# First blocks of the first two layers' projections: two row tiles in banks of their own, turned features ahead of the last early step, and the weight chunk split behind the first features

## The reference

```python
def rms_norm(x, gain):
    y = xf * lax.rsqrt(jnp.mean(xf * xf, axis=-1, keepdims=True) + EPS)
    return (y * gain).astype(x.dtype)

def modulate(x, gain, shift, scale):
    return rms_norm(x, gain) * (1 + scale) + shift
...
    h_l = modulate(x, norm_mix[i], mod_l[0], mod_l[1])
    h_c = modulate(ctx, norm_mix[i], mod_c[0], mod_c[1])
    # i == 0: even_mixer (gated linear attention and attention), i == 1: odd_mixer
    m_l, m_c = even_mixer(h_l, h_c, ev_w_in[j], ev_w_out[j], ...)
    x = x + mod_l[2] * m_l
```

## Time and profile before

| | before |
|---|---|
| median of 3 runs | 1868.26 us (1864.27 to 1869.49) |
| profiled execution | 1866.97 us, of which the span is 1865.1 us |
| PE busy | 1662.8 us, 89% of the span |
| DVE busy | 1117.2 us, 60% |
| ACT busy | 1037.8 us, 56% |
| DMA | 348.05 MB, mean 187 GB/s |
| early modulation (start to `mod_ready`) | 0 to 37.84 us |
| first block of in0 starts | 47.52 us |
| out0 starts | 375.11 us |
| first block of in1 starts | 747.75 us |

### The profile page before, as it was taken

One profiled execution on the slowest core, in us unless ns is written; L12 is line 12 of the kernel. 1 busy time (PEld: TensorE's weight loads), 2 busy tenths in 40 slices (PEclk: granted clock), 3 DMA queues, 4 the chain that ended last, 5 costly groups with the idle time before them and its releaser, 6 DMA issues.

```text
span 1865.1 us, 22644 instructions
## 1 busy us (share of the span) xinstructions
PE 1662.8 (89%) x8804; PEld 1273.4 (68%) x8804; DVE 1117.2 (60%) x1746; ACT 1037.8 (56%) x1865; POOL 155.3 (8%) x157
## 2 busy tenths in 40 slices
PE   4998789897899993899899999988999899999988
PEld 2776447774677772767677777757878667777766
DVE  1225685435688886774589996436754565355453
ACT  4224326625688884385677765526655546446573
POOL 1000100003000003100004331000010010000000
PEclk9999879998899996999899999996999989999999
DMA  8345688012999994301487773530055214414511
GB/s 333 136 157 190 228 335 349 1 68 96 349 422 421 422 387 191 114 1 46 172 322 294 286 288 110 195 138 1 1 190 184 110 49 173 173 68 170 183 65 46
DMA packets 54425, 348.05 MB, mean 187 GB/s; under 512 B 5680, under 2 KB 5680, under 8 KB 18480
## 3 DMA queue, kind: packets, MB, share of 16 engines
q1 hardware_dynamic: 48128, 323.15, 45.6%
q0 software_dynamic: 6192, 23.46, 3.2%
HBM read 317.23 MB, written 29.36 MB: 186 GB/s over the span
## 4 chain that ended last, share of the span: by engine, by line
PE 64%; DVE 15%; ACT 11%; DMA 6%; issue 2%; POOL 1%; SPq 0%; POOLq 0%; DVEq 0%; ACTq 0%
PE bank L1402 15%; PE bank L1404 14%; PE bank L1403 14%; DMA ring_float<-weights_dram 5%; DVE ring_float32r L2891 3%; PE bank L1435 2%; ACT ring_high L725 2%; DVE ring_float32r L2384 2%; DVE Z_float32r L2891 2%; PE bank L1632 1%; ACT hT_float L773 1%; ACT arena_float L860 1%; PE bank L1621 1%; PE bank L1786 1%; PE bank L1916 1%
## 5 line engine op out<-in xcount | busy, mean ns | idle before, releaser
L2384 DVE TENSOR_TENSOR ring_float32r<-ring_float,ring_high 128x1024 fp32r<-128x1024 f32 x206 | 245.5, 1227 | 309.3 <-ACT ring_high L725 308.9
L725 ACT ACTIVATE ring_high<-ring_float 128x1024 fp32r<-128x1024 f32 x206 | 209.4, 1061 | 272.1 <-DMA ring_float<-weights_dram 270.2
L1402 PE MATMUL bank<-ring_high,x_float32r 128*128 128x512 f32 x608 | 242.2, 398 | 6.3 <-DVE mix_float32r L2423 3.3
L1403 PE MATMUL bank<-ring_float32r,x_float32r 128*128 128x512 f32 x608 | 238.7, 393 | 0.0
L1404 PE MATMUL bank<-ring_high,mix_float32r 128*128 128x512 f32 x576 | 226.4, 393 | 0.0
L2891 DVE TENSOR_TENSOR ring_float32r<-ring_float,ring_high 128x1024 fp32r<-128x1024 f32 x122 | 154.4, 1312 | 31.2 <-ACT ring_high L880 31.2
L1402 PE MATMUL bank<-ring_high,arena_float32r 128*128 128x512 f32 (+1 forms) x404 | 156.5, 387 | 18.4 <-DVE arena_float32r L2413 5.1
L2891 DVE TENSOR_TENSOR Z_float32r<-Z_float,arena_float32r 128x1024 fp32r<-128x1024 f32 x126 | 163.0, 1338 | 12.6 <-ACT arena_float32r L880 12.3
L1404 PE MATMUL bank<-ring_high,arena_float32r 128*128 128x512 f32 (+1 forms) x404 | 153.7, 381 | 0.0
L1403 PE MATMUL bank<-ring_float32r,arena_float32r 128*128 128x512 f32 (+1 forms) x404 | 153.4, 380 | 0.0
L1402 PEld LDWEIGHTS bank<-ring_high,x_float32r 128*128 128x128 f32 x608 | 114.1, 188 | 40.1 <-issue 5.2
(11 more groups left out here) (421 smaller groups left out, 3196.2 us busy)
## 6 DMA issues: line engine op xcount, KB each, us to landing
ring_float<-weights_dram SPq DMA_DIRECT2D x216, 1024.0 KB, 4.8
Z_float<-weights_dram SPq DMA_DIRECT2D x63, 1024.0 KB, 7.5
sent<-post_row SPq DMA_DIRECT2D x1, 11776.0 KB, 39.2
Z_float<-sent SPq DMA_DIRECT2D x23, 512.0 KB, 9.1
made<-mix_float POOLq DMA_DIRECT2D x21, 512.0 KB, 7.9
post_row<-norm_post_dram POOLq DMA_DIRECT2D x4, 512.0 KB, 4.5
small<-small_dram SPq DMA_DIRECT2D x1, 1072.0 KB, 9.1
x_float<-x_dram SPq DMA_DIRECT2D x1, 1024.0 KB, 5.3
```

What stands on the lines that cost most here:

```text
L725: nc.scalar.activation(ring_high[:, slot, half], ring[:, slot, half], ACT.Copy).then_inc(high_ready, 1)
L1402: nc.tensor.matmul(out, left[0], right[0], start=start, stop=False)
L1403: nc.tensor.matmul(out, left[0], right[1], start=False, stop=False)
L2384: ve.tensor_tensor(ring_low[:, slot, half], ring[:, slot, half], ring_high[:, slot, half], ALU.subtract).then_inc(low_ready, 1)
```

## The change

- `lead_pool`: in the first block of a projection with four row tiles, tiles 0 and 1 go to `CARRY` (banks 6 and 7) and tiles 2 and 3 to `A`. This holds for in0, out0 and in1.
- `project` takes a bank just ahead of a tile's first product, in all blocks of all projections.
- `mod_early`: eight `dense` products ahead of the first step and five behind each step. The first four feature turnings are issued ahead of the last step, and the other four stay behind the last turn.
- ACT copies the first step's result ahead of the last row tile's normalization, and splits the first chunk of in0 behind the first features rather than ahead of them. DVE splits it likewise behind the first low part.

```diff
+        def lead_pool(n, T, t):
+            return CARRY if n == 0 and T == NT and t < 2 else A
...
-            def drain(*copies, func=ACT.Copy):
-                b = A.filled_bank(act)
+            def drain(*copies, func=ACT.Copy, pool=A):
+                b = pool.filled_bank(act)
...
-                i.then_inc(a_free, 1)
+                i.then_inc(pool.free, 1)
...
                     n.then_inc(a_free, 1)
+                    if j == 0 and between:
+                        between()
...
-                            drain((dst(t), lambda b, w=w: b[:, 0:w], scale(t), None))
+                            drain((dst(t), lambda b, w=w: b[:, 0:w], scale(t), None), pool=lead_pool(n, T, t))
...
+                if i == 0:
+                    mod_copy(mod_rows_early, 1)
                 normed(NT - 1)
                 if i == 0:
-                    mod_copy(mod_rows_early, MOD_EARLY)
+                    mod_copy(mod_rows_early, MOD_EARLY - 1)
                     seen.next(mod_ready)
-                    chunk_high(STREAM["in0"][0])
-                modulate(i, 0, NT, "first")
+                modulate(i, 0, NT, "first", (lambda: chunk_high(STREAM["in0"][0])) if i == 0 else None)
...
             def mod_early():
                 pe.wait_ge(mod_cleared, 1)
-                for _ in range(MOD_EARLY):
+                keep_active(bank[7], 8)
+                for n in range(MOD_EARLY):
+                    if n == MOD_EARLY - 1:
+                        seen.next(normed_ready, NT)
+                        transposes(mix, NT, 0, 4)
                     mod_step(mod_rows_early)
+                    keep_active(bank[7], 5)
                 mod_turn(mod_rows_early).then_inc(mod_turned, 1)
...
-                    banks = [A.take(pe) for _ in range(tiles)]
+                    pools = [lead_pool(n, tiles, t) for t in range(tiles)]
+                    banks = []
                     rows_per = KT // (w // 256)
                     for k0 in range(0, KT, rows_per):
                         last = k0 + rows_per == KT
                         high, low = split_chunk(rows_per)
                         for t in range(tiles):
+                            if k0 == 0:
+                                banks.append(pools[t].take(pe))
...
                             if last:
-                                i.then_inc(a_full, 1)
+                                i.then_inc(pools[t].full, 1)
...
-                seen.next(normed_ready, NT)
-                transposes(mix, NT)
+                    transposes(mix, NT, 4)
+                else:
+                    seen.next(normed_ready, NT)
+                    transposes(mix, NT)
...
                 project("first", T, [(T, 512)] * 2)
+                CARRY.drained(pe)
                 keep_active(bank[6], 20)
...
-            def features_low(name, T):
+            def features_low(name, T, between=None):
...
                         signal(ve.tensor_tensor(low[:, ks, :], hT[:, ks, :], high[:, ks, :], ALU.subtract), act_low)
+                    if j == 1 and between:
+                        between()
...
-                        dve.wait_ge(a_free, whole["y", i, n, t])
+                        dve.wait_ge(*whole["y", i, n, t])
...
-                if i == 0:
-                    chunk_low(first)
-                features_low("first", NT)
+                features_low("first", NT, (lambda: chunk_low(first)) if i == 0 else None)
```

More of the change, by code:

```diff
@@ L754, in normed, with features @@
                 nc.scalar.activation(mix[:, t, :], x[:, t, :], ACT.Copy, scale=rstd[:, t:t + 1]).then_inc(normed_ready, 1)
-            def features(T, scale_bias=None, split=None):
+            def features(T, scale_bias=None, split=None, between=None):
                 per = 4 // T
@@ L991, in route_exps, with modulate @@
                     nc.scalar.activation(src[:, 0:4 * T], src[:, 0:4 * T], ACT.Exp).then_inc(route_out, 1)
-            def modulate(i, which, T, split=None):
-                features(T, lambda k, s: (modA[:, i, which, k, s:s + 1], modT[:, 48 * i + 24 * which + k, s:s + 1]), split)
+            def modulate(i, which, T, split=None, between=None):
+                features(T, lambda k, s: (modA[:, i, which, k, s:s + 1], modT[:, 48 * i + 24 * which + k, s:s + 1]), split, between)
             def first_layer(i):
@@ L1035, in after @@
                 def after(n, t):
-                    whole["y", i, n, t] = A.drains
+                    pool = lead_pool(n, T, t)
+                    whole["y", i, n, t] = pool.free, pool.drains
                     if n == 0 and t == T - 1:
@@ L1457, in mod_late, with transposes @@
                     mod_step(mod_rows_late)
-            def transposes(src, T):
+            def transposes(src, T, first=0, last=KT):
                 per = 4 // T
-                for j in range(KT // per):
+                for j in range(first // per, last // per):
                     b = A.take(pe)
```

## The result

The kernel took 1852.91 us after the change (median of 8 runs, 1849.41 to 1858.59), and 1864.26 us before it (8 runs, 1857.61 to 1869.49, three of them known to the forecast). The ratio is 0.9942, 95% interval 0.9924 to 0.9961: 11.4 us are gained, 7 to 14 by the interval. The profiled execution has a span of 1850.1 us where it was 1865.1. Of the experiments' runs one of e1 took 3219.74 us, where its five others took 1850.73 to 1853.41, and it is in none of the ratios.

The account below looks back on a forecast made before the run. The prediction took PE as the bound, where it idles or runs at its lower clock. Gains of 3.4 + 1.8 + 1.9 + 0.9 + 1.2 = 9.2 us from 1866.97 gave 1857.8, stated as 1858, range 1853.5 to 1863.

Parts of the forecast that it names:

- Early modulation: Steps before in0: dense products raise the clock sooner and the DMA allows the faster steps; 3.4 us gained.
- The third rival: Early steps: chunks land as late as before, only block starts gain; sum 5.8 us, 1861.2 us; chance 0.12.
- Start of in0: From mod_ready to the end of the first chunk's products: earlier products, slow clock stretch left in; 1.8 us gained.
- the slow stretch: Behind a block's start: PE at the lower clock level for a while, costing 1.7 us; left in by the forecast.
- Start of out0: First block of out0: PE goes on when its turnings end; 1.9 us gained, up to 3.6 without slow stretch.
- its second block: Out0's second block: no more wait for ACT to drain the fourth tile; 0.9 us gained.
- Start of in1: First block of in1: 2.4 us gained without a slow stretch, 0.7 with it; 1.2 us taken.
- The first rival: Block starts: short waits keep the clock low, costing 1.7 us at three places; 1862.9 us; chance 0.13.
- The fifth rival: In0 and out0: their slow stretches vanish too, 1.6 + 1.7 us more gained; 1854.5 us; chance 0.13.

Follow-up runs that it names:

- e1: Changed kernel without the early-modulation edits and the chunk's new place; banks 6 and 7 and the late bank take kept: 1852.59 us, ratio 0.9927.
- e8: The changed kernel run again, nothing altered: 1851.28 us, ratio 0.9918.
- e6: Changed kernel with in0's first chunk split ahead of the features again, as before: 1853.54 us, ratio 0.9927.
- e3: Kernel before with only the bank take moved to just ahead of each tile's first product, all in pool A: 1852.17 us, ratio 0.9925.
- e11: Kernel before with only the bank take moved, all in pool A, run a second time: 1852.97 us, ratio 0.9917.
- e5: Kernel before with eight dense products in the idle time ahead of in0, out0 and in1, banks taken as before: 1863.34 us, ratio 0.9986.
- e12: The kernel before, profiled a second time, nothing altered: 1861.38 us.
- e4: Changed kernel without its 28 dense products in the early modulation: 1851.5 us, ratio 0.9918.
- e9: Kernel before with the bank take moved, four turnings ahead of the last early step and the early copy, no dense products: 1850.66 us, ratio 0.9914.
- e10: Kernel before with the bank take moved and six dense products ahead of in0 and in1: 1854.01 us, ratio 0.9917.
- e2: Changed kernel with the early edits kept, but four banks taken ahead of each block in pool A as before: 1863.0 us, ratio 0.998.
- e7: Changed kernel computing only one of four thin products per early half step, sums incomplete: mod_ready at 36.45 us, no whole time given.

## Why the prediction was right or wrong

**Early modulation, 3.4 us: wrong.** This is the step that failed, by the largest amount. It measured 0.4 (37.84 to 37.47), and even that is no more than the scatter of `mod_ready` among profiles with the same code up to there (36.67 to 38.66 over seven). The failing sentence is "The DMA allows it: ... six more at 2.4 to 2.6 us". The chunks came every 2.8 to 3.2 us (15.75, 21.34, 27.45, 33.91, two chunks between each). The rate was read at 14 to 16 us, among loads that had all been issued at the start, and carried over to chunks that each wait for a slot. There 333 to 368 GB/s were seen over ten microseconds before and 340 to 348 after, and only here and there more (407 from 14 to 24 us in e8). Neither bound of the term allowed for this, and why the rate is lower there stays open. The third rival, that chunks land as late as before, came true with a reason that its text did not have: it let the DMA's full share speak for it, and the share was indeed 0.91 after and 0.97 before from 24 to 34 us. The clock did rise, at 14.8 us where the forecast had 15.5.

**Start of in0, 1.8 us: right in size** (2.05, from 22.52 to 20.47), with the slow stretch kept as chosen. The chunk's low part was to end 7.3 us behind `mod_ready`, and PE waited for it until 7.2 behind. What the forecast didn't ask is whether the chunk's new place was worth having. Split first, in0 gains 3.5 (e6), or 4.2 to 4.5 without the other early edits too (e1, e3, e11). By the first product the new place costs 0.7. The rest of these differences is the slow stretch, which reaches further into the products in the kernel after.

**Start of out0, 1.9, and its second block, 0.9: the place right, the size short.** The first product came 2.1 sooner and the second block's wait is gone, but the two kernels differ by 4.5 (52.73 less 48.24, with the missing record). The rest is the slow stretch, 1.7 in the forecast's account and 1.35 by e5. The forecast had priced it nearly rightly (1.9, 0.9 and 1.7 make 4.5) and let it stay; it went. That is the second step that failed.

**Start of in1, 1.2: short by the same.** The whole block gained 2.50. The forecast had 2.4 for a start without a slow stretch, and that is what came. So over out0 and in1 it is 3.0 us short.

**The first rival, a clock that falls in small waits,** did not come in the kernel after, with waits of 0.32 us in in1's first tile and a clock of 1.00 from 740 us on in both of its profiles. It did come once in ten profiles with an early `take`, in e1, for 1.3 us at one place where the forecast had 1.7 at three. The Trainium skill (TensorE: Matmul & The Clock Gate, "A second HAM failure mode") tells of a clock that swings behind short idles between groups. One fall like it was seen here in ten profiles, and none in the kernel after.

**The fifth rival** came half: of the two that it names, out0's stretch vanished and in0's stayed, and in1's, which it doesn't name, vanished as well. So the stages gave 0.4 + 2.05 + 4.5 + 2.5 = 9.4 us in the profile. That this is near the forecast's 9.2 is luck: 3.0 us too much in the early modulation stand against 3.2 too little at the starts.

**The base.** The forecast took these from 1866.97, the profiled execution. That was 3 us above a usual one in a stretch far from the change (e12), and above the 1864.26 of the result's 8 runs of before. (The median of the three runs known then, 1868.26, was higher still.) 1864.26 less 9.4 would be 1854.8, 1.9 above what was measured. So the forecast missed its range for the base, 2.7 too high, and for these 1.9, and not for its sum. The medians of the experiments differ by more than the stages explain: 12.2 to 17.0 us for e1, e3, e4, e6, e8, e9, e10 and e11, where the sums over in0, out0 and in1 are 9 to 11.5. No stage of their profiles has another gain in common beside that of 1170 to 1330 us, which all but e9 have, and e2, e5 and e12 too. So 2 us of the gain (e3) up to 5 (e8) are not assigned, in e9 over 7, and whose they are stays open. The sets differ by such amounts without the `take` as well: e2 is 2.8 faster with nothing gained at the starts, and e5 is 2.4 faster with 4.5 gained there. Of the 15.0 us between the two profiles' spans, 3.35 are the stretch from 1170 to 1330 us and 3.0 another, from 900 to 1000 us, where the granted clock is 0.95 before and 1.00 after. E8, the same kernel as after, has none of these 3.0. Two single runs of the same kernel differ by 7.7 us (e12).

## What to carry to other kernels

Take a bank just ahead of the product that needs it, not all banks ahead of a block. That move alone gave here as much time as the whole change (1852.17 and 1852.97, against 1852.91 and 1851.28), 11.4 us at the three starts (e3). Of these 4.5 are, by e5, the clock that no longer falls behind an idle PE, and the rest the earlier products and out0's second block. Where a start must wait, a few `dense` products in the wait bring back the clock's part alone (1.35 to 1.56 us a start). Read a DMA rate where loads are issued as in the stage that it is to bound: ten microseconds from 8 us on would have shown 426 GB/s, and ten from 24 on, where each load waits for a slot, 368. Take a forecast's base from the median of more than three runs, with a second profile where stretches far from the change may have been unlucky.

## What the runs showed of the hardware

Idle time of PE ahead of a full stretch is paid twice, and the second part comes later: 1.86 us of idling ahead of out0 brought the clock down not in the gap but behind it, while PE was fully busy (0.57 at 376 to 378 us, 0.58 at 378 to 380, and 1.00 again from 380). Dummy products in the gap gave all of this back (e5). In1's waits of 0.32 us left the clock up in nine of ten profiles, and in one it fell behind them (e1).

Work moved ahead of a wait can cost more than it saves. With half of the turnings gone from behind the last turn, PE was idle for 4.53 us in e9 and had the lower level from 40 to 46 us, and in the kernel after from 38.7 to 48.9 (in e7, with the same turnings moved, only from 39.8 to 43.2); e3, with all turnings behind the turn, had its slow stretch over them and was at the full level from 42 us on, and its in0 was 1.9 us shorter than e9's. The whole times of the two don't show it (1852.17 and 1850.66).

Loads of 1 MB came at 426 GB/s over 10 us while the first of them were all queued (8 to 18 us), and at 421 over 50 us later in the kernel (530 to 580 us). Through three slots, each load issued after its slot came free, the early modulation saw 333 to 368 GB/s over 10 us before, 340 to 348 after, and up to 407 and 409 (e8 and e3).
